# Gathered rows transposed by VectorE in 32x32 blocks instead of by TensorE, in a two-layer decoder with a mixture of experts

## The reference

```python
scores = jax.nn.sigmoid(xf @ w_router)          # 64 experts in 8 groups, the best 8 experts of the best 4 groups
gates = gates / gates.sum(-1, keepdims=True) * ROUTE_SCALE
def block_ffn(args):                            # for the rows of one expert
    xb, e = args
    hdn = jax.nn.silu(xb @ w_gate[e]) * (xb @ w_up[e])      # 1024 -> 256
    return hdn @ w_down[e]                                  # 256 -> 1024
routed = segment_sum(y_rows * row_gate[:, None], row_token) # back to the tokens
h = layer_norm(DN_ALPHA * h + routed + shared, ln2_g, ln2_b)
```

## Time and profile before

| | us |
|---|---|
| median of 3 runs | 1532.04 (1531.19 to 1534.55) |
| profiled execution, device time | 1533.96 |
| profiled execution, span | 1532.2 |
| busy in the span: TensorE / VectorE / ScalarE / GpSimd | 1476.8 / 355.0 / 256.4 / 137.3 |

### The profile page before, as it was taken

One profiled execution on the slowest core, in us unless ns is written; L12 is line 12 of the kernel. 1 busy time (PEld: TensorE's weight loads), 2 busy tenths in 40 slices (PEclk: granted clock), 3 DMA queues, 4 the chain that ended last, 5 costly groups with the idle time before them and its releaser, 6 DMA issues. The chain is left out here.

```text
span 1532.2 us, 21421 instructions
## 1 busy us (share of the span) xinstructions
PE 1476.8 (96%) x8455; PEld 763.7 (50%) x8455; DVE 355.0 (23%) x1113; ACT 256.4 (17%) x611; POOL 137.3 (9%) x163
## 2 busy tenths in 40 slices
PE   8999998999999999999979999989999999999996
PEld 5755454444444544544437545444544545454452
DVE  0431381111111111111143422711111111111112
ACT  1243110111111111111122530101111111111110
POOL 2031012000000000000000210110000000000000
PEclk9997899999999999999989987999999999999998
DMA  9711435999999999999945213359999999999990
GB/s 341 288 62 55 138 114 188 414 405 398 402 404 390 404 405 397 405 404 392 348 151 192 104 62 123 127 220 411 401 417 414 415 413 412 416 412 412 411 406 33
DMA packets 103411, 471.25 MB, mean 308 GB/s; under 512 B 11680, under 2 KB 18016, under 8 KB 70464
## 3 DMA queue, kind: packets, MB, share of 16 engines
q1 hardware_dynamic: 91344, 442.32, 72.6%
q0 software_dynamic: 12016, 28.27, 5.2%
HBM read 484.48 MB, written 3.35 MB: 318 GB/s over the span
## 5 line engine op out<-in xcount | busy, mean ns | idle before, releaser
L600 PE MATMUL bank<-ring,region 128*64 128x256 f32 x4096 | 455.9, 381 | 1.7 <-issue 1.7
L600 PEld LDWEIGHTS bank<-ring,region 128*64 128x64 f32 x4096 | 296.8, 138 | 176.3 <-issue 39.8
L559 PE MATMUL bank<-region 128*128 128x512 f32 x512 | 267.5, 607 | 1.4 <-ACT region L1110 0.7
L638 PE MATMUL bank<-ring,region 128*64 128x512 f32 x1024 | 249.6, 608 | 2.4 <-ACT region L1110 1.4
L1489 DVE TENSOR_TENSOR region<-region,bank 128x256 f32<-128x256 f32 x64 | 27.0, 422 | 558.3 <-ACT region L1103 558.3
L1110 ACT ACTIVATE region<-bank 128x512 f32<-128x512 f32 x128 | 76.5, 598 | 474.5 <-PE bank L638 474.5
L1776 POOL DMA_INDIRECT region<-h_rows,rank_i x64 | 63.8, 997 | 921.5 <-DVE region L1468 865.0
L638 PEld LDWEIGHTS bank<-ring,region 128*64 128x64 f32 x1024 | 62.4, 136 | 162.9 <-issue 86.5
L559 PEld LDWEIGHTS bank<-region 128*128 128x128 f32 x512 | 77.9, 191 | 58.1 <-issue 54.9
L572 PEld LDWEIGHTS bank<-const,region 128*128 128x128 f32 x512 | 66.8, 195 | 69.3 <-ACT region L1094 42.8
L572 PE MATMUL bank<-const,region 128*128 128x128 f32 x512 | 90.6, 299 | 4.1 <-ACT region L1094 2.8
(11 more groups left out here) (197 smaller groups left out, 916.6 us busy)
## 6 DMA issues: line engine op xcount, KB each, us to landing
ring<-in_w_gate_dram SPq DMA_DIRECT2D x64, 2048.0 KB, 10.3
ring<-in_w_up_dram SPq DMA_DIRECT2D x64, 2048.0 KB, 12.7
ring<-in_w_down_dram SPq DMA_DIRECT2D x64, 2048.0 KB, 9.0
ring<-in_w_in_dram SPq DMA_DIRECT2D x8, 2048.0 KB, 17.3
ring<-in_w_o_dram SPq DMA_DIRECT2D x4, 2048.0 KB, 10.9
ring<-in_w_in_dram SPq DMA_DIRECT2D x4, 1024.0 KB, 8.0
ln_par<-in_ln_g_dram POOLq DMA_DIRECT2D x4, 512.0 KB, 5.5
ln_par<-in_ln_b_dram POOLq DMA_DIRECT2D x4, 512.0 KB, 7.7
```

The source lines that it names most:

```text
L559: last = mm(bank[SUM_BANKS[n][half]][0:w, :], selg[:, u, t0:t0 + w], y_sb[:, u, half * 512:(half + 1) * 512], start=False, stop=stop, skip ...
L600: last = mm(bank[5][64 * e:64 * e + 64, part * F:(part + 1) * F], xgT[:, u, kk, 64 * e:64 * e + 64], w[:, e, kk, :], start=(kk == 0), stop ...
L638: last = mm(bank[6][64 * e:64 * e + 64, :], mo["h2"][:, j * 128 + 64 * e:j * 128 + 64 * e + 64], w[:, e, j, half * 512:(half + 1) * 512], ...
```

## The change

The gathered rows are no longer turned by TensorE through bank 7 but by VectorE, whose transpose turns each 32x32 block in place within its 32 partitions. For this, the rows are gathered in quarters: `h_rows` becomes [1088, 256], and gather j of four brings slots 32j to 32j+31 of the pair, with quarter c of each row to the partitions 32c to 32c+31. `rank_i` holds the indices for it, made from 16 small products more in `turn_lists`. The gates lie in a DRAM tensor of their own, `g_rows`, and are gathered by a fifth indirect DMA with the old indices, now `slot_i`. Bank 7 becomes free: y's two halves have a bank each, 6 and 7, and the transposes of h go into bank 5. TensorE no longer waits for a gather; VectorE does. The scatters move: the meta tokens' ahead of the transposes of h, both halves of chunk 2 between these and y.

```diff
-        mo = carve([("xg", 2 * ROW), ("xgT", 2 * 1024), ...
+        mo = carve([("xg", 2 * D), ("xgate", 2 * E), ("xgT", 2 * 1024), ...
-        rank_i = sb("rank_i", [128, PAIRS], I32)
+        rank_i = sb("rank_i", [128, 4, PAIRS], I32)
+        slot_i = sb("slot_i", [128, PAIRS], I32)
-        h_rows = nc.dram_tensor("h_rows", [T, ROW], F32, kind="Internal").ap()
+        h_rows = nc.dram_tensor("h_rows", [4 * T, QUARTER], F32, kind="Internal").ap()
+        g_rows = nc.dram_tensor("g_rows", [T, E], F32, kind="Internal").ap()
...
                 for e in range(2):
-                    last = mm(bank[7][64 * e:64 * e + 64, 0:PAIRS], mo["list"][0:64, :], own[:, e, :], start=True, stop=True)
+                    mm(bank[7][64 * e:64 * e + 64, 0:PAIRS], mo["list"][0:64, :], own[:, e, :], start=True, stop=True)
+                for j in range(4):
+                    for c in range(4):
+                        last = mm(bank[7][32 * c:32 * c + 32, 128 + j * PAIRS:128 + (j + 1) * PAIRS],
+                                  mo["list"][0:64, 32 * (j % 2):32 * (j % 2) + 32], own[:, j // 2, :], start=True, stop=True)
...
                         if not opens:
-                            pe.wait_ge(ht_ready, g * 32 + p)
-                        if not ends:
-                            pe.wait_ge(gathered[1 - u], past * (16 * 16) + ((i + u) * 16 + 16))
-                            turn_x(1 - u, 0)
-                        if not opens:
                             pe.wait_ge(y_ready, g * 64 + p * 2)
                             pe.wait_ge(selg_ready, g * 32 + p)
                             scatter(l, 1 - u, 1, 0)
-                        if not ends:
-                            pe.wait_ge(xta_ready, g * 32 + p + 2)
-                            turn_x(1 - u, 1)
-                        if not opens:
                             scatter(l, 1 - u, 1, 1)
+                            if l == 0:
+                                scatter(l, 1 - u, 0, 0)
                         pe.wait_ge(h_ready, g * 32 + p + 1)
-                        if not ends:
-                            pe.wait_ge(xtb_ready, g * 32 + p + 2)
                         for j in range(2):
-                            last = pe.transpose(bank[7][:, j * 128:(j + 1) * 128], mo["h"][:, j * 128:(j + 1) * 128], ident)
+                            last = pe.transpose(bank[5][:, j * 128:(j + 1) * 128], mo["h"][:, j * 128:(j + 1) * 128], ident)
                         last.then_inc(ht_done, 1)
                         if not opens:
                             scatter(l, 1 - u, 2, 0)
-                            if l == 0:
-                                scatter(l, 1 - u, 0, 0)
+                            scatter(l, 1 - u, 2, 1).then_inc(scattered, 1)
...
-                                    last = mm(bank[6][64 * e:64 * e + 64, :],
+                                    last = mm(bank[Y_BANKS[half]][64 * e:64 * e + 64, :],
...
+                def turned(nth, u):
+
+                    dve.wait_ge(gathered[u], past * (64 * 16) + (nth * 64 + 64))
+                    rows = xg[:, u, :].rearrange("p (j f k) -> p k j f", j=4, k=KC)
+                    dve.transpose(xgT[:, u, :, :].rearrange("p k (j s) -> p k j s", j=4), rows).then_inc(xt_ready, 1)
+
+                def read_gate(q, nth, u):
+                    hold_here(dve, gate_in[u], past * (16 * 16) + (nth * 16 + 16))
...
-                        hold_here(pool, xtb_done, g * 32 + q - 1)
+                        hold_here(pool, xt_ready, g * 32 + q - 1)
+                    for j in range(4):
+                        pool.indirect_dma_start(out=xg[:, u, j * QUARTER:(j + 1) * QUARTER], out_offset=None, in_=h_rows,
+                                                in_offset=bass.IndirectOffsetOnAxis(ap=rank_i[:, j, q:q + 1], axis=0),
+                                                bounds_check=4 * T - 1, oob_is_err=False).then_inc(gathered[u], 16)
+                    if q >= 2:
                         hold_here(pool, gate_read, g * 32 + q - 1)
-                    pool.indirect_dma_start(out=xg[:, u, :], out_offset=None, in_=h_rows,
-                                            in_offset=bass.IndirectOffsetOnAxis(ap=rank_i[:, q:q + 1], axis=0),
-                                            bounds_check=T - 1, oob_is_err=False).then_inc(gathered[u], 16)
+                    pool.indirect_dma_start(out=xgate[:, u, :], out_offset=None, in_=g_rows,
+                                            in_offset=bass.IndirectOffsetOnAxis(ap=slot_i[:, q:q + 1], axis=0),
+                                            bounds_check=T - 1, oob_is_err=False).then_inc(gate_in[u], 16)
```

More of the change, by code:

```diff
@@ L372, in decoder_kernel @@
         h_ready = sem("h_ready")
-        xtb_ready = sem("xtb_ready")
+        xt_ready = sem("xt_ready")
         ht_ready = sem("ht_ready")
         gathered = [sem(f"gathered{i}") for i in range(2)]
+        gate_in = [sem(f"gate_in{i}") for i in range(2)]
         gather_over = sem("gather_over")
@@ L565, in round_, with two_pairs @@
                 g = l * ROUNDS + r
-                past = pe.snap(rounds_run)
-                def turn_x(u, part):
-                    rows = xg[:, u, 0:D].rearrange("s (p k) -> s k p", k=KC)
-                    for j in range(4):
-                        last = pe.transpose(bank[7][:, j * 128:(j + 1) * 128], rows[:, 4 * part + j, :], ident)
-                    last.then_inc((xta_done, xtb_done)[part], 1)
-                pe.wait_ge(gathered[0], past * (16 * 16) + 16)
-                pe.wait_ge(idf_ready, g + 1)
-                turn_x(0, 0)
-                pe.wait_ge(xta_ready, g * 32 + 1)
-                turn_x(0, 1)
-                def two_pairs(i, first=False, final=False):
+                def two_pairs(i, first=False):
                     for u in range(2):
-                        opens, ends = first and u == 0, final and u == 1
+                        opens = first and u == 0
                         p = i * 2 + u
@@ L641, in two_pairs @@
                             last.then_inc(y_done, 1)
-                            if half == 0 and not opens:
-                                scatter(l, 1 - u, 2, 1).then_inc(scattered, 1)
                 two_pairs(0, first=True)
@@ L1031, in _ @@
                     with pe.Else():
[L1032 removed]
+                        for s, per in ((gates_used, 32), (gu_done, 32), (ht_done, 32),
                                        (y_done, 64), (list_turned, 1)):
@@ L1091, in round_, with two_pairs @@
                 g = l * ROUNDS + r
-                def turned(q, u):
-                    act.wait_ge(xta_done, g * 32 + q + 1)
-                    act.activation(xgT[:, u, 0:4, :], bank[7][:, :].rearrange("p (k s) -> p k s", k=4), ACT.Copy)\
-                        .then_inc(xta_ready, 1)
-                def two_pairs(i, first=False, final=False):
+                def two_pairs(i, first=False):
                     for u in range(2):
@@ L1276, in _ @@
                     with act.Else():
-                        for s, per in ((sig_ready, 32), (xta_ready, 32), (y_ready, 64)):
+                        for s, per in ((sig_ready, 32), (y_ready, 64)):
                             act.wait_ge(s, l * (ROUNDS * per) + per)
```

70 lines of the change are left out of this document (32 added, 38 removed).

## The result

The changed kernel took 1514.19 us against 1531.68 us for the kernel before, medians of four runs each, taken side by side; the ratio is 0.988 with a 95% interval of 0.986 to 0.990. (One of the four runs of the changed kernel took 4914.58 us; without it, as in the ratio, the median is 1513.36.) Run again at the end of the study, it took 1521.69 against 1531.49 us, a ratio of 0.994 (0.992 to 0.996). The forecast was 1524, 8 us less than before. The first measurement has 17.5 us less, the second 10. So direction and bound were right; in the first measurement the gain was more than twice what was forecast, in the second it was close to it.

The account below looks back on a forecast made before the run. TensorE (16.44 us a pair, layer 0) and DMA (16.0, layer 1) nearly level; afterwards DMA binds at 16.5. Layer 0 -14, layer 1 +2.3, its start +3.5 make -8.2 us: 1525.8 profiled, 1524 median; range 1503 to 1552.

Parts of the forecast that it names:

- the slack of 12 and 18 us: Last up weights land 12 us before use in layer 1, 18 us in layer 0, largely limiting TensorE's gain.
- TensorE's saving: Eight transposes fewer save TensorE 1.19 us a pair, 74 us in all; TensorE as bound after all, 1460 us: chance 0.02.
- The block transpose: On VectorE, 1.28 us, at most 2.6, hidden; slow rival from about 2.7 us, at 5.1 us 126 us slower: chance 0.06.
- The second bank: Separate bank for y's second half costs nothing, as that half already ran behind a scatter covering the evacuation.
- The DMA's pace in layer 1: 16.0 + 0.5 = 16.5 us a pair; loads land 14.3 us later, 12 of it slack, so 2.3 us slower.
- the price of the gathers: Quartered gathers and gates' gather cost the DMA 0.5 us a pair, between 0.35 (576 more packets) and 0.99.
- fixed part for each DMA: Each gather costs 0.16 us besides its packets; if it comes five times, 0.64 us more a pair.
- Layer 0: Last up weights land 2 us later, TensorE is 16 us earlier; 14 us gain taken for its loop.
- The starts of the loops: Layer 1's first gate product about 4.8 us later, TensorE idle some 7 us, loads shifted 3.5 us; layer 0: 0.
- Dear gathers: Rival: the fixed 0.16 us comes with each DMA, 0.99 us a pair, 28 us more, 1552 us; chance 0.27.
- Free gathers: Rival: small packets slip between the large ones; layer 0 wins 30 us, layer 1 8, 1494 us; chance 0.07.
- The falling clock: Rival: TensorE's clock falls with idle waits of about 1 us a pair, costing 2 to 6 us, 1528; chance 0.08.

Follow-up runs that it names:

- half loads: Either kernel with weight loads past each layer's first two pairs bringing only half of each row: before 1533.32 us (1.000), changed 1449.39 us (0.947).
- no gathers: Either kernel without its gathers, their semaphores raised by GpSimd: before 1529.93 us (0.998), changed 1443.57 us (0.943).
- 4.0 us of transposes: Changed kernel with VectorE doing each block transpose twice, first into a spare buffer: 1575.69 us (1.026).
- Gathers of nothing: Changed kernel with all five gathers of a pair issued but the bound set to row 0, so every index above it is skipped: 1463.41 us (0.953).

## Why the prediction was right in its bound and wrong in its size

**The bound: right.** TensorE's pace, the slack of 12 and 18 us in the ring, and so that TensorE's saving would mostly not come out, all came from the earlier trace rows, and the runs bear it out: half loads and no gathers change 0 to 4 us before and 63 to 69 after.

**TensorE's saving: a little small, without effect.** I had 15.25 and 14.70 us a pair; half loads show 15.05 and 14.45. By the ratios 82 us are there and not 74. The last pair, from which I read 1.19 us, showed less than the 1.4 that a pair saves. In TensorE's timelines the eight transposes take 1.07 us of a pair. The rest comes from the new order: the four scatters go from 3.91 to 3.73 us and the two halves of y from 3.64 to 3.48 where they run without others between them, and the last pair of the kernel before still has y's halves apart. The loads hide the difference.

**The block transpose: wrong value, inside its bounds.** 2.04 us, not 1.28. The nearest row, an elementwise operation over as many elements without a stride, was not near enough; the measured value is 1.6 times that. The text had given 2.6 as the upper bound and found even that hidden behind the DMA, so the forecast did not suffer. With 4.0 us of transposes TensorE waits 1.25 us in layer 0, so its cover is 2.7 us. In layer 1, without the small scatters of the meta tokens, it is 2.1, and the real transpose fits by 0.1; I had found that 1.28 just fits. The limit of "about 2.7 us", from which on TensorE's pace was to pass the DMA's 16.5, was too low: with 4.0 us most of its steps take 16.3 or 16.4. The Trainium skill (Vector Engine (DVE) Microarchitecture Reference, The reshape front-end and per-opcode configuration) has one element per cycle per lane for a transpose; this trace does not bear it out for four-byte elements read with a stride of 32 bytes, which took 1.6 times as long as an elementwise operation over as many. Whether the transpose or the stride costs it, no run tells apart.

**The second bank: right by the rows, for a reason I gave wrongly.** In the time of the changed kernel no difference is shown without it, with 2 to 3 us more in layer 0's loop of one profile. But I said that a scatter covers y's second half already. The change moves that scatter ahead, and the bank replaces it as cover; where the loads don't bind, it is worth 50 to 55 us.

**The DMA's pace in layer 1: this is the step that failed.** The sum took 16.0 + 0.5 = 16.5 us a pair, so that layer 1's last weights would land 14.3 us later, 2.3 more than the slack of 12, and its loop would be longer. The landings go at 16.2 us, so they come about 29 x 0.23 = 6.7 us later, the slack takes them, and the loop is 5.7 us shorter instead. That is 8 of the 12.5 us between the forecast's -8.2 and the -20.7 of the profiled runs. Both terms of the 16.5 were too large.

The 0.5 us was the price of the gathers, between 0.35 for 576 more packets and 0.99 with a fixed part for each DMA. The count was wrong: 80 more packets a pair and not 576 (224 against 144), which at the same price of 0.0006 us are 0.05 us. I had multiplied the 144 packets of a gather by the number of gathers, as if a place of the list were always a packet. It is one only as long as the row fills it; cut into quarters, four places share one, and a further gather adds just its own 16. The earlier trace rows held the 144, and 128 places plus 16 would have been legible in it; what a smaller piece does no row of before could show, and there I should have set a lower bound near nothing. The fixed part, 0.16 us by the remainder of a difference, is 0.05 to 0.11 for each further gather of rows and 0.09 to 0.15 for that of the gates. Together the four further DMAs cost about 0.35 to 0.4 us a pair: 0.27 for the quartering (16.23 against 15.96 us with one gather) and 0.09 to 0.15 for the gates. That this is near the bound of 0.35 is luck, since the packets that it was made of are not there.

The 16.0 us I had called what the DMA needs. It is only an upper bound. The same two landings in the kernel before without its gathers, and in the changed kernel with one gather of rows:

```profile
1017.24 0.37 SPq L436 DMA_DIRECT2D ring<-in_w_down_dram  x1
ring<-in_w_down_dram SPq DMA_DIRECT2D x1, 2048.0 KB, 7.9
...
1477.88 0.37 SPq L436 DMA_DIRECT2D ring<-in_w_down_dram  x1
ring<-in_w_down_dram SPq DMA_DIRECT2D x1, 2048.0 KB, 10.5
```

```profile
998.08 0.37 SPq L439 DMA_DIRECT2D ring<-in_w_down_dram  x1
ring<-in_w_down_dram SPq DMA_DIRECT2D x1, 2048.0 KB, 9.5
...
1446.71 0.75 SPq L439 DMA_DIRECT2D ring<-in_w_down_dram  x1
ring<-in_w_down_dram SPq DMA_DIRECT2D x1, 2048.0 KB, 23.8
```

The first has 16.0 us a pair too, though a pair's loads alone take 15.06 when they set the pace (the changed kernel without gathers): here they follow TensorE, which frees a slot every 15.9 us. In the kernel before, the time to landing stays at 8.8 to 9.7 us up to pair 20 and grows only behind it. The second kernel's loads do set the pace, at 15.96 us with the gates' own gather in it, so the kernel before needs some 15.8 to 15.9 (an estimate from runs of different jobs). From there to 16.23 is the real price of the change; the sum only had to reckon from the 16.0 that was seen, and so needed 0.23.

Layer 0 came out as forecast, in the time at which its loop ends: 14.4 us earlier (253.9 + 510.3 against 257.1 + 492.7), for a forecast of 14. Its last up weights land at 746.0, 3.6 us later than before, where I had 2, and TensorE takes them at once.

```profile
719.24 3.71 SPq L439 DMA_DIRECT2D ring<-in_w_up_dram  x1
ring<-in_w_up_dram SPq DMA_DIRECT2D x1, 2048.0 KB, 26.8
```

That hides two errors that cancel, a head 3.2 us longer and a loop 3.6 us shorter than I had. The rest of the 12.5 us: the start of layer 1 came 1.9 us later and not 3.5, and the tail is 2.6 us shorter, which nothing in the change explains.

**The starts of the loops: near in sum for layer 1, missed in layer 0.** For layer 1 I had the first gate product 4.8 us later behind the list's products. The timeline of the changed kernel:

```profile
983.98 0.30 PE L551 MATMUL bank<-const,region 64*64 64x32 f32 x4
984.22 0.46 PE L554 MATMUL bank<-const,region 64*32 64x32 f32 x32
...
986.25 1.09 POOL L1754 DMA_INDIRECT region<-h_rows,rank_i  x1 [19.67 <-issue]
...
990.28 1.00 POOL L1754 DMA_INDIRECT region<-h_rows,rank_i  x1 [0.30 <-issue]
...
994.59 9.06 PE L592 MATMUL bank<-ring,region 128*64 128x256 f32 x64 [6.29 <-DVE region L1439]
```

From the list's products to the first gate product it is 994.59 - 983.98 = 10.6 us, where the kernel before has 8.1: 2.5 later. The 32 products took 0.46 us, not the 2.4 that I scaled from four: 28 more of them add 0.16 us to the 0.30 of four, so products that small overlap. The gap, 6.29 us, is near the 7 that I named. In layer 0 I had put 0, because TensorE still works on the shared expert while the gathers run. The work was too short: 0.39 us of idle time ahead of the first gate product in the first run, 3.41 in the later one, and slow products after it.

```profile
247.92 8.13 PE L592 MATMUL bank<-ring,region 128*64 128x256 f32 x57 [3.41 <-DVE region L1439]
256.85 0.65 PE L592 MATMUL bank<-ring,region 128*64 128x256 f32 x3 [0.80 <-issue]
258.26 0.38 PE L592 MATMUL bank<-ring,region 128*64 128x256 f32 x1 [0.76 <-issue]
```

The head is 3.2 us longer than before in the first run, 6.8 in the second, 5.4 in the kernel before with four gathers, and not longer with one gather (252.2) or two (252.7). So the four gathers cost 3 to 7 us here in these runs; other kernels with four have heads of 254.9 to 264.6 us, and the spread is not explained. In the later run the head and layer 1 are why the whole gained only 9.8 us. That this is near the forecast's 8 is luck, for its layer 0 loop ends 10.2 us earlier and not 14, and its layer 1 loop is 2.5 us shorter and not longer.

**The rivals.** Dear gathers had 0.27 and were refuted, by the pace and by one, two and four gathers. Free gathers had 0.07 and are refuted too, by the 13.5 us that quartering costs in the loops. The falling clock had 0.08. It is real, in one or two of 31 steps of layer 1 (the 18.8 above, with a granted clock of 0.97 over those 50 us) and at the starts of the loops. Whether it makes the distance between the two runs of the changed kernel is not shown; that distance lies in the head, with 3.6 of 7.8 us, and in layer 1, with 3.2.

**What stays open.** Why the same kernel takes 1514 us in one job and 1522 in another, be it by the chip or not, while the kernel before agrees to 0.2 us in the two: the segments say where, not why. The tail, unchanged code, has 21 to 24 us in runs of either kernel without a pattern that I can name, and 2.6 us between the two profiled runs are such a difference. If the medians hold it too, the first comparison's gain is about 15 without it.

## What to carry to other kernels

When two resources are within some per cent of each other, work taken off one is worth only the slack that lies in the buffers of the other plus the small difference of their paces; halve the other's load in an experiment to see what the saving would be without it. The pace at which loads land is what the DMA needs only where the time from issue to landing keeps growing or an engine waits for the loads; else it is the pace of whoever frees the slots. Before pricing DMAs by their packets, look at what a packet of the present queue holds: small pieces may share one. The first pass of a loop waits for all that its later passes hide, so price it by itself.

## What the hardware showed unexpectedly

The block transpose of 128x1024 fp32 takes 2.04 us on VectorE, against 1.28 for an elementwise operation over as many elements. In layer 1, with a wait of 1.9 us in each round of TensorE, the granted clock stayed up after some waits and fell after others, in 12 of 31 rounds (0.81 and 0.85 in stretches of 5 us); in layer 0, with a wait of 1.25 us in rounds as long, it did not fall between 271 and 786 us. Gathers of nothing cost the DMA 0.38 us a pair (pace of the loads 15.06 against 15.44 us) though their packets took 1.0% of the engines' time, or about 0.16 us a pair (0.5 us of 50, for three pairs): they cost more than twice what the view of the queue shows. And the 16 landings of one load ran 14 us apart at the end of a loop, and under 6 us with the gathers' filled places dealt out in turn.
